# PEER gates inside the activation products: two fp32r products of a split one-hot, two one-hot buffers instead of four

## The chip, the cores and the metric

The kernel runs on one core of one Trainium2 chip. The metric is the device time of one execution in microseconds. The engines are TensorE (PE, with its weight loads as PEld), VectorE (DVE), ScalarE (ACT), GpSimd (POOL) and SyncE (SP), whose queue issues most DMAs.

## What is computed

Two transformer blocks over 256 tokens of width 1024. The change touches the last part alone, the PEER layer of the second block. Cut to that, and written densely as the kernel does it:

```
q  = xn @ w_q                                   # 256 tokens, 8 heads, 2 halves of 128
top 16 of 128 keys per half, top 16 of the 16 x 16 sums per head
idx = i * 128 + j,  gate = softmax(best scores) # 128 experts for each token
act = einsum("cd,ced->ce", xc, u[ic])           # u: 16384 x 1024
hid = gelu(act) * gate
out = einsum("ce,ced->cd", hid, v[ic])          # v: 16384 x 1024
x   = x + out ; rmsnorm(x, norm_f_g)
```

The kernel doesn't gather. It computes `gelu(u @ xn)` for all 16384 experts, keeps it as `A[i, j, token]` (partition i, 128 j, 256 tokens), multiplies it with a dense gate matrix G[i, j, token] that is zero but for the 128 chosen experts, and multiplies the product with all of v. G of one token is a product over the 128 choices k: `sum_k onehot_i[k, i] * gate[k] * onehot_j[k, j]`.

## The kernel before

**Streams.** u and v are each streamed in 64 chunks of 1 MB (`PEER_CHUNKS`, two j of the 128: `CJ = 2`) through three buffers `raw`. The products run in fp32r, so a chunk is split: `lead` is the chunk rounded to fp32r (two buffers), `rest` is what is left (in place, over `raw`). A u chunk takes 48 matmuls of 256 columns on PE: for each of two j, 8 with `nT_hi` and 8 with `nT_lo` on `lead` (L1706), then 8 with `nT_hi` on `rest` (L1710). PE increments `chunk_used` at the chunk's end. ACT turns the bank into gelu values in `A` (L1260, `act_ready`).

**While DVE routes.** DVE does the top-k of the routing during the first `ROUTING = 16` chunks. For these ACT makes `lead` (L1266) and POOL makes `rest` (L974). From chunk 16 on DVE makes both (L2179, L2187). Between chunk 15 and 16 PE waits for DVE's `gates_ready` and turns gates and indices (L1724), which DVE copies into `bestT` and `ijT` (L2190 to L2192, `route_ready`). ACT's exp of the best scores (L1280) stands in ACT's order behind its share of the 16 chunks.

**The gate stage.** It begins when all 64 u chunks are done. The tokens are taken in 64 groups of 4 (`GT`, `GROUPS`), with four buffers `hot` (`HOTS = 4`). For a group, DVE makes the one-hots of j, and in each fourth group those of i too (L2199); ACT makes the other one-hots of i as `relu(1 - (i - iota)^2)` (L1292 four times, L1296). POOL copies four gates (L988) and multiplies the one-hots of j with them (L991). PE does 4 exact fp32 products of 128 columns (L1739; the profile shows 8 records for them), and DVE multiplies the bank into `A` for the group's 4 tokens (L2206, 512 elements a partition).

**The v products** begin when all groups are done (`gated`): 64 chunks, each with 24 matmuls of 512 columns (L1766). DVE makes `lead` and `rest` of v, and `hid_hi` and `hid_lo` of the two columns of `A` (L2230). Then DVE adds the four banks to `h` (L2254), the last norm follows, and the output is stored.

All orders are written out by hand, one in-order queue per engine, held together by semaphores.

Of the kernel before, what the change touches and what calls it, by code (L numbers as in the profile page):

```python
# [27 lines left out]
P = 128  # L28
T = 256
# [65 lines left out]
ROUTING = 16  # L95
# [4 lines left out]
HOTS = 4  # L100
VECTOR_HOTS = 1
SCALAR_HOTS = HOTS - VECTOR_HOTS
# [62 lines left out]
def build(nc, dram, out):  # L165
    with ExitStack() as ctx:
# [21 lines left out]

        h = keep("h", [P, NT, D])
# [180 lines left out]
        bestT = at("bestT", [P, T], WORK + 3072)  # L370
        ijT = at("ijT", [P, 2, T], WORK + 4096)
        hot = [at(f"hot{b}", [P, 2, GT, NKEYS], ARENA + 24576 + 4096 * b) for b in range(HOTS)]
# [7 lines left out]
        cur_g = keep("cur_g", [P, HOTS, GT])  # L380
# [52 lines left out]
        ws_masked = sem("ws_masked")  # L433
# [95 lines left out]
        chunk_used = sem("chunk_used")  # L529
        act_ready = sem("act_ready")  # L530
# [5 lines left out]
        cur_ready = sem("cur_ready")  # L536
# [4 lines left out]
        gain_f_in = sem("gain_f_in")  # L541
# [228 lines left out]
        QUERY_BANK = [4, 5, 6, 7, 0, 1, 2, 3]  # L770
        def fill(i, at_n):

            return 16 * (at_n // RAW_SLOTS + 1) + 16 * (UNROLL // RAW_SLOTS) * i
# [7 lines left out]
        def _(sp):  # L781
# [93 lines left out]
            sp.dma_start(keysT[:, :, :], dram["keysT"].rearrange("c (a n) -> c a n", n=NKEYS)).then_inc(keys_in, 16)  # L875

# [24 lines left out]
            sp.dma_start(gain_f[:, :], dram["norm_f_g"].broadcast_to([P, D])).then_inc(gain_f_in, 16)  # L901
# [7 lines left out]
        def _(pool):  # L909
# [6 lines left out]
            pool.memset(w_sT[CHUNK:P, :, 0:CHUNK], 0.0).then_inc(ws_masked, 1)  # L916

            pool.wait_ge(ws_masked, 1)
# [57 lines left out]

            for n in range(ROUTING % UNROLL):
                pool_rest(n, n)
            with pool.Fori(0, ROUTING // UNROLL) as i:
                for s in range(UNROLL):  # L980
                    at_n = ROUTING % UNROLL + s
                    pool_rest(at_n + UNROLL * i, at_n)

            pool.wait_ge(route_ready, 1)

            def weigh_hot(g, b):
# [7 lines left out]
            with pool.Fori(0, GROUPS // HOTS) as turn:  # L994
                for b in range(HOTS):
                    weigh_hot(HOTS * turn + b, b)
# [3 lines left out]
        def _(act):  # L1000
# [256 lines left out]
            def act_column(n, at_n):  # L1257
                act.wait_ge(chunk_used, n + 1)
                dst = A[:, bass.ds(n * CJ, CJ), :].rearrange("p j t -> p (j t)")
                act.activation(dst, bank[4 + at_n % 2][:, :], ACT.Gelu).then_inc(act_ready, 1)  # L1260
# [6 lines left out]

            head = ROUTING % UNROLL
            for n in range(head):
# [3 lines left out]
            with act.Fori(0, ROUTING // UNROLL) as i:  # L1273
                for s in range(UNROLL):
                    at_n = head + s
# [5 lines left out]
            with act.Fori(ROUTING // 2 - 1, PEER_CHUNKS // 2) as n2:  # L1281
                for b in range(2):
                    act_column(2 * n2 + b, b)

            act.wait_ge(route_ready, 1)

            def scalar_hots(turn, b, peeled):
                k = SCALAR_HOTS * turn + b - VECTOR_HOTS
                if not peeled:
                    act.wait_ge(gates_done, HOTS * (turn - 1) + b + 1)  # L1290
                for t in range(GT):
                    last = act.activation(hot[b][:, 0, t, :], c("iota")[:, 0:NKEYS], ACT.Square,  # L1292
                                          bias=ijT[:, 0, bass.ds((HOTS * turn + b) * GT + t, 1)], scale=-1.0)
                last.then_inc(hot_i_step, 1)
                act.wait_ge(hot_i_step, 2 * k + 1)
                act.activation(hot[b][:, 0, :, :], hot[b][:, 0, :, :], ACT.Relu, bias=1.0,  # L1296
                               scale=-1.0).then_inc(hot_i_step, 1)

            for b in range(VECTOR_HOTS, HOTS):
                scalar_hots(0, b, True)  # L1300
            with act.Fori(1, GROUPS // HOTS) as turn:
                for b in range(VECTOR_HOTS, HOTS):
                    scalar_hots(turn, b, False)
# [4 lines left out]
        def _(pe):  # L1308
# [43 lines left out]
            pe.wait_ge(ws_masked, 1)  # L1352
# [333 lines left out]
            def bank_free(n, peeled):  # L1686
                if not peeled or n >= 2:
                    pe.wait_ge(act_ready, n - 1)

# [5 lines left out]
            def act_split(n, at_n, peeled=False):  # L1695

                slot, b = at_n % RAW_SLOTS, at_n % 2
                bank_free(n, peeled)
                hi = columns_of(lead[b], "u")
                lo = columns_of(rest[slot], "u")  # L1700
                pe.wait_ge(lead_ready, n + 1)
                for j in range(CJ):
                    dst = bank[4 + b][:, j * T:(j + 1) * T]
                    for x in (nT_hi, nT_lo):
                        for k in range(KD):
                            pe.matmul(dst, hi[:, k, j, :], x[:, k, :], start=(x is nT_hi and k == 0), stop=False)  # L1706
                    if j == 0:
                        pe.wait_ge(rest_ready, n + 1)
# [608 lines left out]
```

## Time and profile before

| | |
|---|---|
| median of 3 runs | 1921.12 us (1920.65 to 1923.58) |
| the profiled execution | 1920.95 us, span of the trace 1919.2 us |
| PE busy | 1662.7 us (87%) |
| DVE busy | 1301.7 us (68%) |
| ACT busy | 706.9 us (37%) |
| POOL busy | 451.9 us (24%) |
| the chain that ended last | PE 35%, DVE 7%, issue 3%, POOL 3% |

The time of an execution is the span and about 1.8 us around it. In a timeline row the first number is the start in the span, the second the length, then engine, line, operation, tiles, shapes and count; what stands in brackets is the idle time before it and what ended it. Rows of one engine may overlap by some hundredths to tenths of a microsecond, since an instruction begins before the one ahead has left the pipeline.

### The profile page before, as it was taken

The page shows a single profiled execution, that of the slowest core. Times are in us where ns is not written, and L with a number is a line of the kernel's source. Part 1 is how long each engine was busy: PE and PEld are TensorE (multiplying, and loading weights), DVE is VectorE, ACT ScalarE, POOL GpSimd, SP SyncE. Part 2 cuts the span into 40 slices and gives each one's busy share as a digit, 9 for nine tenths or more (in the row PEclk, how much of TensorE's full clock was granted, in tenths as well). Part 3 has the DMA queues.
Part 4 walks back from the last instruction along what each step waited for, and adds up shares of the span by engine and source line. Part 5 has one row for each costly group of instructions (what it writes and reads, how often), then busy time and mean ns, then how long its engine had stood idle before and what let it go on. Part 6 is the DMA issues. An engine that isn't in the chain of part 4 may idle for free. (4 is left out here: it accounts for less than half of the span.)

```text
span 1919.2 us, 25753 instructions
## 1 busy us (share of the span) xinstructions
PE 1662.7 (87%) x9316; PEld 1331.6 (69%) x9316; DVE 1301.7 (68%) x1434; ACT 706.9 (37%) x929; POOL 451.9 (24%) x257
## 2 busy tenths in 40 slices
PE   6986998788887877788989959999996679999997
PEld 6855555444444536677678959999995568888886
DVE  3345887777777734855216996666659988888887
ACT  4514776666666624243233422222237720000000
POOL 5602111111111105532135840000019930000000
PEclk9996899999999988797999989999999989999999
DMA  8416999999999985421412533555550015555554
GB/s 282 144 50 259 367 397 397 396 396 396 396 396 397 397 324 149 173 89 47 158 37 111 176 131 132 185 187 178 192 176 0 0 66 197 195 188 189 194 196 142
DMA packets 142119, 406.90 MB, mean 212 GB/s; under 512 B 11128, under 2 KB 14328, under 8 KB 125560
## 3 DMA queue, kind: packets, MB, share of 16 engines
q1 hardware_dynamic: 136408, 395.77, 57.3%
q10 hardware_dynamic: 5664, 10.49, 1.5%
q8 instruction: 32, 0.52, 0.1%
q14 instruction: 15, 0.12, 0.0%
HBM read 396.80 MB, written 10.35 MB: 212 GB/s over the span
## 5 line engine op out<-in xcount | busy, mean ns | idle before, releaser
L1983 DVE TENSOR_TENSOR ring_rest<-ring,w_lead 128x2048 fp32r<-128x2048 f32 x128 | 291.7, 2320 | 86.1 <-ACT w_lead L1110 86.0
L1110 ACT ACTIVATE w_lead<-ring 128x2048 fp32r<-128x2048 f32 x128 | 237.8, 1904 | 92.2 <-DMA ring<-in_w_gate 42.9
L2187 DVE TENSOR_TENSOR rest<-raw,lead 128x2048 fp32r<-128x2048 f32 x112 | 256.8, 2293 | 3.9
L2179 DVE CAST lead<-raw 128x2048 fp32r<-128x2048 f32 x112 | 137.4, 1227 | 153.3 <-PE bank L1710 98.9
L711 POOL TENSOR_TENSOR ring_rest<-ring,half_lead 128x2048 fp32r<-128x2048 f32 (+1 forms) x38 | 172.5, 4554 | 233.6 <-ACT half_lead L705 233.5
L1513 PE MATMUL bank<-w_lead,x_two 128*128 128x512 f32 x512 | 154.6, 438 | 56.2 <-ACT w_lead L1110 49.1
L616 ACT ACTIVATE xhat<-h 128x1024 f32<-128x1024 f32 x6 | 6.3, 1056 | 457.0 <-DVE h L2254 360.7
L1513 PE MATMUL bank<-ring_rest,x_two 128*128 128x512 f32 x512 | 149.0, 419 | 29.3 <-DVE ring_rest L1983 29.1
L1513 PEld LDWEIGHTS bank<-w_lead,x_two 128*128 128x128 f32 x512 | 93.7, 200 | 115.8 <-ACT w_lead L1110 87.3
L1766 PE MATMUL bank<-lead,hid_hi 128*128 128x512 f32 x512 | 158.8, 392 | 5.5 <-DVE hid_lo L2230 5.5
L1766 PE MATMUL bank<-rest,hid_hi 128*128 128x512 f32 x512 | 158.6, 391 | 0.0
L1766 PE MATMUL bank<-lead,hid_lo 128*128 128x512 f32 x512 | 158.4, 391 | 0.0
L1706 PE MATMUL bank<-nT_hi,lead 128*128 128x256 f32 x1024 | 145.6, 285 | 4.9 <-ACT lead L1266 2.6
L1513 PEld LDWEIGHTS bank<-ring_rest,x_two 128*128 128x128 f32 x512 | 98.2, 201 | 72.0 <-DVE ring_rest L1983 52.3
L1710 PE MATMUL bank<-nT_hi,rest 128*128 128x256 f32 x1024 | 143.5, 283 | 5.0 <-POOL rest L974 5.0
L1706 PE MATMUL bank<-nT_lo,lead 128*128 128x256 f32 x1024 | 142.4, 281 | 0.0
L954 POOL TENSOR_TENSOR x_two<-x_blk,x_two 128x512 fp32r<-128x512 f32 x32 | 42.4, 1324 | 422.9 <-ACT x_two L1148 422.9
L1706 PEld LDWEIGHTS bank<-nT_hi,lead 128*128 128x128 f32 x1024 | 133.6, 194 | 5.5 <-issue 2.7
L1710 PEld LDWEIGHTS bank<-nT_hi,rest 128*128 128x128 f32 x1024 | 130.6, 189 | 6.0 <-POOL rest L974 6.0
L991 POOL TENSOR_TENSOR hot<-hot,cur_g 128x512 f32<-128x512 f32 x64 | 68.1, 1064 | 282.4 <-DVE hot L2199 277.4
L1706 PEld LDWEIGHTS bank<-nT_lo,lead 128*128 128x128 f32 x1024 | 131.5, 191 | 0.0
L1468 PE MATMUL bank<-ring,hT 128*64 128x512 f32 x512 | 116.9, 598 | 1.4 <-issue 1.4
(317 smaller groups left out, 2710.5 us busy)
## 6 DMA issues: line engine op xcount, KB each, us to landing
ring<-in_w_gate SPq DMA_DIRECT2D x32, 2048.0 KB, 19.7
ring<-in_w_up SPq DMA_DIRECT2D x32, 2048.0 KB, 22.6
ring<-in_w_down SPq DMA_DIRECT2D x32, 2048.0 KB, 20.2
raw<-in_u SPq DMA_DIRECT2D x64, 1024.0 KB, 4.9
raw<-in_v SPq DMA_DIRECT2D x64, 1024.0 KB, 4.9
ring<-in_w_in SPq DMA_DIRECT2D x14, 2048.0 KB, 11.8
ring<-in_w_out SPq DMA_DIRECT2D x4, 2048.0 KB, 7.8
y_sorted<-y_blk ACTq DMA_DIRECT2D x64, 128.0 KB, 5.4
```

The costliest lines, as they stand in the source:

```text
L711: pool.tensor_tensor(half_view(ring_rest[slot], i, half), half_view(ring[slot], i, half), half_lead(i, half).bitcast(F32), ALU.subtract).t ...
L954: pool.tensor_tensor(x_two[j][:, :, BLOCK:], x_blk[j][:, :, :], x_two[j][:, :, 0:BLOCK].bitcast(F32), ALU.subtract).then_inc(x_lo_ready, 1)
L991: pool.tensor_tensor(hot[b][:, 1, :, :], hot[b][:, 1, :, :], spread(cur_g[:, b, :].unsqueeze(2), [P, GT, NKEYS]), ALU.mult).then_inc(hot_j ...
L1110: act.activation(w_lead[half][:, :, :], ring8(slot)[:, 4 * half:4 * half + 4, :], ACT.Copy).then_inc(w_lead_ready, 1)
L1468: last = pe.matmul(dst[half * BLOCK:(half + 1) * BLOCK, :], hidden_t[:, f, :], ring4(w)[:, f, half * 512:(half + 1) * 512], start=(f == 0) ...
L1513: last = pe.matmul(bank[2 * kind + j][:, :], x_two[j][:, 4 * half + k, :], part[:, k, :], start=(ready is w_lead_ready and half == 0 and k ...
L1706: pe.matmul(dst, hi[:, k, j, :], x[:, k, :], start=(x is nT_hi and k == 0), stop=False)
L1710: last = pe.matmul(dst, lo[:, k, j, :], nT_hi[:, k, :], start=False, stop=(k == KD - 1))
L1766: ins = pe.matmul(bank[2 * half + t][:, :], x[b][:, j, tok], v[:, j, half * 512:(half + 1) * 512], start=(first and j == 0 and i == 0), st ...
L1983: dve.tensor_tensor(ring_rest8(slot)[:, part, :], ring8(slot)[:, part, :], w_lead[half][:, :, :].bitcast(F32), ALU.subtract).then_inc(w_re ...
L2179: return dve.tensor_copy(dst, src)
L2187: dve.tensor_tensor(rest[slot][:, :], raw[slot][:, :], lead[b][:, :].bitcast(F32), ALU.subtract).then_inc(rest_ready, 1)
```

## The change

`ROUTING` goes from 16 to 24; POOL makes the rests of 25 chunks (`POOL_RESTS`). ACT makes `lead` for all 64 u chunks, and DVE only `rest` from chunk 25 on. The separate gate stage is gone: chunks 25 to 62 each carry one or two groups (`groups_in`: 12 chunks with one, 26 with two) between their two halves on PE. The one-hots are fp32r, in two buffers. The gates are split too, `best_hi` and `best_lo`; POOL makes two weighted one-hots per group (`hot_hi` and `hot[:, 1]`), and PE does 8 fp32r products of 128 columns where it did 4 fp32 ones. Four banks hold gates, three hold activations.

A column of `A` that isn't computed yet when a group's gates come takes the gates themselves (`tensor_copy`); columns that are there are multiplied. When a later chunk's activations come, ACT writes gelu back into the bank for tokens that already have gates, and DVE multiplies them in (`mix_columns`). The `hot` buffers lie over `h`, so `h` is written to DRAM (`h_kept`, 1 MB) before and read back after the last gates; the load of `gain_f` moves to the end of the u products.

```diff
-ROUTING = 16
+ROUTING = 24
+POOL_RESTS = ROUTING + 1
-HOTS = 4
+HOTS = 2
+GATE_BANKS = 4
+FIRST_MIXED = POOL_RESTS
+LAST_MIXED = PEER_CHUNKS - 2
+def groups_through(n):
+    spans = LAST_MIXED - FIRST_MIXED + 1
+    return min(max(n - FIRST_MIXED + 1, 0), spans) * GROUPS // spans
+def groups_in(n):
+    return range(groups_through(n - 1), groups_through(n))
...
 # sync
+            sp.dma_start(h_kept, h[:, :, :].rearrange("p t d -> p (t d)")).then_inc(h_saved, 16)
...
+            sp.wait_ge(gates_done, GROUPS)
+            sp.wait_ge(h_saved, 16)
+            sp.dma_start(h[:, :, :].rearrange("p t d -> p (t d)"), h_kept).then_inc(final_in, 16)
+            sp.wait_ge(chunk_used, PEER_CHUNKS)
+            sp.dma_start(gain_f[:, :], dram["norm_f_g"].broadcast_to([P, D])).then_inc(final_in, 16)
...
 # gpsimd
-                pool.tensor_copy(cur_g[:, b, :], bestT[:, bass.ds(g * GT, GT)]).then_inc(cur_ready, 1)
-                pool.wait_ge(cur_ready, g + 1)
                 pool.wait_ge(hot_ready, g + 1)
-                pool.tensor_tensor(hot[b][:, 1, :, :], hot[b][:, 1, :, :],
-                                   spread(cur_g[:, b, :].unsqueeze(2), [P, GT, NKEYS]), ALU.mult).then_inc(hot_j_ready, 1)
+                pool.tensor_tensor(hot_hi[b][:, :, :], plain, spread(best_hi[:, tok].bitcast(F32).unsqueeze(2), wide),
+                                   ALU.mult)
+                pool.tensor_tensor(hot[b][:, 1, :, :], plain, spread(best_lo[:, tok].bitcast(F32).unsqueeze(2), wide),
+                                   ALU.mult).then_inc(hot_j_ready, 1)
...
 # scalar
+            for n in range(ROUTING - 1, PEER_CHUNKS):
+                if n + 1 < PEER_CHUNKS:
+                    act.wait_ge(chunk_used, n)
+                    act_lead(n + 1, n + 1, fill(0, n + 1))
+                act_mixed_column(n - 1)
...
+                for g in groups_in(n + 1):
+                    if not vector_makes_both(g):
+                        scalar_hot(g)
...
 # tensor
-                    last = pe.matmul(bank[4 + b][:, t * NKEYS:(t + 1) * NKEYS], hot[b][:, 0, t, :], hot[b][:, 1, t, :],
-                                     start=True, stop=True)
+                    pe.matmul(dst, hot[b][:, 0, t, :], hot_hi[b][:, t, :], start=True, stop=False)
+                    last = pe.matmul(dst, hot[b][:, 0, t, :], hot[b][:, 1, t, :], start=False, stop=True)
                 last.then_inc(gates_done, 1)
...
+            for n in range(ROUTING, PEER_CHUNKS):
...
+                act_half_chunk(n, n, 0)
+                for g in groups_in(n):
+                    gate_products(g)
+                act_half_chunk(n, n, 1).then_inc(chunk_used, 1)
...
 # vector
+            def gate_columns(g, n):
...
+                dve.tensor_copy(A[:, ready:, tok], gates[:, ready:, :])
+                dve.tensor_tensor(A[:, 0:ready, tok], gates[:, 0:ready, :], A[:, 0:ready, tok], ALU.mult).then_inc(gated, 1)
+            def mix_columns(n):
...
+                dve.tensor_tensor(view, pair_of(n)[:, :, 0:done], view, ALU.mult).then_inc(columns_mixed, 1)
...
+            for n in range(FIRST_MIXED, PEER_CHUNKS):
+                if n + 1 < PEER_CHUNKS:
+                    rest_of(n + 1)
+                if n > FIRST_MIXED:
+                    mix_columns(n - 1)
+                else:
+                    dve.wait_ge(act_ready, n)
+                for g in groups_in(n + 1):
+                    one_hots(g)
+                for g in groups_in(n):
+                    gate_columns(g, n)
```

The next two pieces are PE's order where the gates are made. Before, it is the end of the u products: the last half chunk, then the first gate products and the loop over the other groups.

```order
L1706 MATMUL bank<-nT_hi,lead_202 128x256 x8
L1706 MATMUL bank<-nT_lo,lead_202 128x256 x8
L1710 MATMUL bank<-nT_hi,rest_198 128x256 x8
L1726 REGISTER_ALU
L1726 COMPARE_AND_BRANCH
L1739 MATMUL bank<-hot_207 128x128 x4
L1739 MATMUL bank<-hot_208 128x128 x4
L1739 MATMUL bank<-hot_209 128x128 x4
L1739 MATMUL bank<-hot_210 128x128 x4
```

Now, chunk 25, the first with a group (`hot_hi_210` is the upper part of the weighted one-hots, `hot_208` holds the one-hots of i and the lower part):

```order
L1752 MATMUL bank<-nT_hi,rest_199 128x256 x8
L1783 MATMUL bank<-hot_hi_210,hot_208 128x128
L1784 MATMUL bank<-hot_208 128x128
L1783 MATMUL bank<-hot_hi_210,hot_208 128x128
L1784 MATMUL bank<-hot_208 128x128
L1783 MATMUL bank<-hot_hi_210,hot_208 128x128
L1784 MATMUL bank<-hot_208 128x128
L1783 MATMUL bank<-hot_hi_210,hot_208 128x128
L1784 MATMUL bank<-hot_208 128x128
L1748 MATMUL bank<-nT_hi,lead_202 128x256 x8
```

The group's eight products stand between the two halves of the chunk, and the second half can't begin before them.

DVE's order in the u products. Before, for each chunk from 16 on, and in the gate stage for each group:

```order
L2179 CAST lead_202<-raw_195 128x2048
L2187 TENSOR_TENSOR rest_198<-raw_195,lead_202 128x2048
```

```order
L2206 TENSOR_TENSOR A<-bank,A 128x128x4
L2199 ISA
L2199 TENSOR_TENSOR hot_208<-const,ijT 128x512
```

Now one turn in the middle of the u products, with two groups made ready for the next chunk and two gated of the present one:

```order
L2245 TENSOR_TENSOR rest_200<-raw_197,lead_202 128x2048
L2275 TENSOR_TENSOR A<-bank,A 128x2x20
L2254 TENSOR_TENSOR hot_208<-const,ijT 128x512
L2254 TENSOR_TENSOR hot_209<-const,ijT 128x512
L2266 COPY A<-bank 128x72x4
L2267 TENSOR_TENSOR A<-bank,A 128x56x4
```

The rest of the next chunk comes first in each turn, before the one-hots.

## Rows read from the trace of the kernel before

**Rows 1.** Busy time of each engine by stage, the view of windows
```profile
core 0: us, PE busy (x) PEld busy (x) DVE busy (x) ACT busy (x) POOL busy (x), PEclk, DMA share, GB/s
1035.00:1157.10 122.10, 95.71 (x775) 94.13 (x775) 117.81 (x363) 40.71 (x35) 82.10 (x17) 0.91 0.41 138
1157.10:1433.00 275.90, 275.86 (x2304) 275.65 (x2304) 167.63 (x95) 58.95 (x71) 0.00 (x0) 0.99 0.52 179
1433.00:1558.00 125.00, 80.86 (x512) 69.98 (x512) 120.53 (x133) 91.42 (x243) 111.62 (x127) 0.91 0.02 8
1558.00:1909.10 351.10, 351.05 (x1536) 290.12 (x1536) 286.35 (x252) 0.00 (x0) 0.00 (x0) 0.99 0.54 184
```
**Rows 2.** The end of the routing, timeline of DVE and POOL
```profile
1116.77 2.29 DVE L2162 TENSOR_TENSOR match<-const,bdigf 128x2048 f32<-128x2048 f32 x1
1119.10 6.56 DVE L2165 TENSOR_TENSOR match<-match,tif 128x2048 f32<-128x2048 f32 x1
1125.69 2.29 DVE L2166 TENSOR_REDUCE ij<-match 128x128 f32<-128x2048 f32 x1
1128.01 4.27 DVE L2162 TENSOR_TENSOR match<-const,bdigf 128x2048 f32<-128x2048 f32 x1
...
1117.01 13.11 POOL L974 TENSOR_TENSOR rest<-raw,lead 128x2048 fp32r<-128x2048 f32 x2 [1.08 <-ACT lead L1266]
```
**Rows 3.** The same stretch, timeline of PE
```profile
1130.17 1.21 PE L1710 MATMUL bank<-nT_hi,rest 128*128 128x256 f32 x8 [0.65 <-POOL rest L974]
...
1153.24 0.69 PE L1724 MATMUL bank<-const,best 128*128 128x128 f32 x2 [19.00 <-DVE best L2175]
...
1157.10 2.08 PE L1706 MATMUL bank<-nT_hi,lead 128*128 128x256 f32 x8 [2.31 <-DVE lead L2179]
...
1161.73 1.12 PE L1706 MATMUL bank<-nT_hi,lead 128*128 128x256 f32 x8
...
1164.59 1.12 PE L1706 MATMUL bank<-nT_hi,lead 128*128 128x256 f32 x8
```
**Rows 4.** One turn of the gate stage, timeline of all engines
```profile
1500.63 1.13 PE L1739 MATMUL bank<-hot 128*128 128x128 f32 x8 [0.91 <-POOL hot L991]
1500.73 1.26 ACT L1292 ACTIVATE hot<-const,ijT 128x128 f32<-128x128 f32 x4
1500.86 0.68 DVE L2206 TENSOR_TENSOR A<-bank,A 128x512 f32 x1
1501.06 1.04 POOL L991 TENSOR_TENSOR hot<-hot,cur_g 128x512 f32<-128x512 f32 x1
1501.45 1.19 DVE L2199 TENSOR_TENSOR hot<-const,ijT 128x512 f32<-128x512 f32 x1
1502.03 0.63 ACT L1296 ACTIVATE hot<-hot 128x512 f32<-128x512 f32 x1
```
**Rows 5.** Instructions by tile, ns min/median/max: the tile hot
```profile
L2199 DVE TENSOR_TENSOR hot<-const,ijT x64: 677/1192/1726, 1433.1 to 1547.5; 128x512 f32<-128x512 f32 x48, 128x1024 f32<-128x1024 f32 x16
```
**Rows 6.** Groups by line and shape, busy us and mean ns
```profile
L2187 DVE TENSOR_TENSOR rest<-raw,lead 128x2048 fp32r<-128x2048 f32 x112 | 256.8, 2293 | 3.9
L954 POOL TENSOR_TENSOR x_two<-x_blk,x_two 128x512 fp32r<-128x512 f32 x32 | 42.4, 1324 | 422.9 <-ACT x_two L1148 422.9
L1266 ACT ACTIVATE lead<-raw 128x2048 fp32r<-128x2048 f32 x16 | 30.4, 1908 | 0.0
```
**Rows 7.** Narrow matmuls of the MoE part, timeline of PE
```profile
400.61 1.10 PE L1454 MATMUL bank<-const,hid 64*128 64x64 f32 x8
```
**Rows 8.** End of the u products, timeline of all engines
```profile
1431.85 1.11 PE L1710 MATMUL bank<-nT_hi,rest 128*128 128x256 f32 x8
1433.06 3.87 DVE L2199 TENSOR_TENSOR hot<-const,ijT 128x1024 f32<-128x1024 f32 x4 [7.86 <-PE bank L1710]
```
**Rows 9.** Begin and end of the v products, timeline of all engines
```profile
1558.04 1.19 PE L1766 MATMUL bank<-lead,hid_hi 128*128 128x512 f32 x2 [5.52 <-DVE hid_lo L2230]
...
1909.13 2.48 DVE L2254 TENSOR_TENSOR h<-bank,h 128x512 f32<-128x512 f32 x4 [6.01 <-PE bank L1766]
```

More of the change, by code:

```diff
@@ L99, with vector_makes_both @@
 GROUPS = T // GT
-HOTS = 4
-VECTOR_HOTS = 1
-SCALAR_HOTS = HOTS - VECTOR_HOTS
+HOTS = 2
[7 more added lines that the diff above has]
+    return range(groups_through(n - 1), groups_through(n))
+def vector_makes_both(g):
+    return g % 4 == 0
+SCALAR_TURN = {g: k for k, g in enumerate(g for g in range(GROUPS) if not vector_makes_both(g))}
 PAIR = [(0, 0), (0, 1), (0, 2), (1, 0), (1, 1), (1, 2)]
@@ L1280, in _, with act_mixed_column @@
             act.activation(best[:, :, :], best[:, :, :], ACT.Exp).then_inc(best_exp, 1)
[L1281 to L1290, printed above, removed]
+            def act_mixed_column(n):
+                done = GT * groups_through(n)
+                act.wait_ge(chunk_used, n + 1)
+                pair = pair_of(n)
+                if done < T:
+                    last = act.activation(A[:, n * CJ:(n + 1) * CJ, done:], pair[:, :, done:], ACT.Gelu)
+                if done:
+                    last = act.activation(pair[:, :, 0:done], pair[:, :, 0:done], ACT.Gelu)
+                last.then_inc(act_ready, 1)
@@ L1294, in scalar_hots @@
                 last.then_inc(hot_i_step, 1)
                 act.wait_ge(hot_i_step, 2 * k + 1)
-                act.activation(hot[b][:, 0, :, :], hot[b][:, 0, :, :], ACT.Relu, bias=1.0,
+                act.activation(hot[b][:, 0, :, :], hot[b][:, 0, :, :].bitcast(F32), ACT.Relu, bias=1.0,
                                scale=-1.0).then_inc(hot_i_step, 1)
[L1299 to L1303, printed above, removed]
+            for n in range(ROUTING - 1, PEER_CHUNKS):
[3 more added lines that the diff above has]
+                act_mixed_column(n - 1)
+                if n + 1 == FIRST_MIXED:
+                    act.wait_ge(h_saved, 16)
+                    act.wait_ge(route_ready, 1)
+                for g in groups_in(n + 1):
+                    if not vector_makes_both(g):
+                        scalar_hot(g)
@@ L1713, in _, with act_chunk @@
+            def act_chunk(n, at_n, peeled=False):
+                if not peeled or n >= 3:
+                    pe.wait_ge(act_ready, n - 2)
+                act_half_chunk(n, at_n, 0)
+                act_half_chunk(n, at_n, 1).then_inc(chunk_used, 1)
             pe.wait_ge(score_ready, 8)
-            for n in range(ROUTING % UNROLL):
-                act_split(n, n, True)
-            with pe.Fori(0, ROUTING // UNROLL) as i:
+            for n in range(UNROLL):
+                act_chunk(n, n, True)
@@ new lines, in _, with rest_of, one_hots @@
+            dve.tensor_copy(ijT[:, 0, :], bank[ROUTE_BANK[0]][:, T:])
+            dve.tensor_copy(ijT[:, 1, :], bank[ROUTE_BANK[1]][:, 0:T]).then_inc(route_ready, 1)
+            def rest_of(n):
+                slot, b = n % RAW_SLOTS, n % 2
+                dve.wait_ge(lead_ready, n + 1)
+                dve.tensor_tensor(rest[slot][:, :], raw[slot][:, :], lead[b][:, :].bitcast(F32), ALU.subtract).then_inc(rest_ready, 1)
+            def one_hots(g):
+                b = g % HOTS
+                first = 0 if vector_makes_both(g) else 1
@@ L2213, in _ @@
[L2213 to L2223 removed]
+                if n > FIRST_MIXED:
+                    dve.wait_ge(columns_mixed, n - FIRST_MIXED)
```

172 lines of the change are left out of this document (84 added, 88 removed).

## The prediction

> **What bounds the kernel now.** I read the chain that ended last first, and then cut the PEER part into its stages with the view of windows [rows 1]. In the u products from chunk 16 on and in the v products PE is busy for all of the stretch, at full clock: these two stages are PE's own time. The two others are not. In the gate stage (1433 to 1558) PE is busy for 81 of 125 us, while DVE has 120.5 and POOL 111.6: DVE and POOL set it, some 1.9 us for each of 64 groups. In the routing stage PE has 95.7 of 122.1 us: the timeline of PE shows that it finished its 16 chunks at about 1134 (1130.17 and 32 matmuls) and sat for 19 us until DVE's routing was through [rows 3]. So there are two things to win, the idle part of the routing and the gate stage, and the change goes for both.
>
> Two prices of PE come from here. The half chunks begin 2.86 us apart (1161.73, 1164.59) [rows 3]: 24 matmuls of 256 columns at 0.119 us, 5.71 us a chunk. The v products take 351.1 us for 64 chunks, and 10.1 us follow them [rows 9].
>
> **A lock between DVE and POOL.** In the timelines DVE's operations with two operands in SBUF and POOL's don't overlap in substance. L2165 alone is a 2.3 us operation like L2162; it took 6.56 us when POOL had just begun a rest, and POOL's two rests took 13.1 us between them [rows 2]. In the gate stage a one-hot of DVE took 1.19 us beside POOL's multiply, and the same takes 0.68 where POOL is idle [rows 4, 5]. L2206, which reads PSUM and one SBUF operand, keeps its 0.68 us beside POOL, and L2166, with one operand, its 2.29 [rows 2, 4]. So each waits for the whole instruction of the other. The Trainium skill says so too (SBUF: State Buffer, Who interferes with whom: an exclusive lock, the second one blocks fully, and a VectorE instruction with at most one SBUF input doesn't contend); the trace agrees, and as a rule it speaks against this change, which puts DVE's rests and POOL's multiplies into the same stretch.
>
> **Routing, 24 chunks.** Before, chunk 16 starts at 1157.1 [rows 3]. Now PE goes on to chunk 23 before the turn. But POOL's rests go on too, beside DVE's last 2-input operations. At 1132.3 (1128.01 and 4.27) five of these are left, three L2165 and two L2162; the reduction L2166 runs under a rest. One rest and one such operation take 6.6 us together (from the end of L2165 at 1125.7 to 1132.3, or 13.1 over two), so some 4.5 for the rest. Five turns bring DVE to 1165.5, the last L2166 to 1167.8, and the small subtraction waits for the next rest until 1170.0. PE in this time gets a rest each 6.6 us in place of 5.7: those of chunks 16 to 21 end at 1136.8 to 1170.0. 22 follows at 1174.9 and 23 at 1180.9 (its lead waits for chunk 21, at 1173.8, and takes 0.5 for the gelu before it and 1.9 us [rows 6]). A chunk ends 3.8 us or more after its rest came, chunk 22 at 1179.5 and chunk 23 at 1185.2. ACT's exp now stands behind the lead of chunk 23, near 1177, and DVE's gates are ready at about 1182, hidden behind chunk 23. With 1.6 us for the turn chunk 24 starts at 1186.8. Eight chunks more have then cost 29.7 us in place of 45.7: 16 us won. Without any waits for POOL it would be 1181.
>
> **The gates on PE.** What a fp32r product of 128 columns costs no row shows. From below: the slope between 256 columns (0.119) and 512 (351.1 / 1536 = 0.229) leaves 0.064. But the 64-column matmuls of the MoE part, with a full 128-column weight load for each, start (1.10 - 0.27) / 7 = 0.118 us apart, where 0.27 is one of them to its end [rows 7]: a floor by the weight load. From above: eight records of L1739 take 1.13 us in a row [rows 4], 0.12 apart, and these are exact products in two records each; if a narrow fp32r product cost as much as an exact one, a group would be 1.9 to 2.3 us. I take the floor, 8 x 0.119 = 0.95 us, since L1454 is the same limit with still fewer columns. The Trainium skill would have less (TensorE: Matmul & The Clock Gate, Back-to-back issue gap: about 81 ns for a pair of load and matmul with 128 columns); by it 64 groups would be 41 us and not 61, and the whole up to 19 us shorter, less what then waits for POOL. No run here shows it. PE's own sum: 40 chunks x 5.71 = 228.2, and 64 x 0.95 = 60.9: 289.1 us.
>
> **Do the others keep up?** A chunk has 6.66 us with one group and 7.61 with two. ACT: lead 1.9, gelu 0.8, two times 1.26 and 0.63 [rows 4, 6]: 6.5 us, enough. DVE: rest 2.2, one-hots 0.6 each, gates 0.7 per group in two instructions (533 ns of elements, as L2206), columns 0.2 to 0.6: some 5.4. POOL: four multiplies. The nearest row is L991 with 1.04 us, the same multiply with the same broadcast operand and a plain f32 result [rows 4]; L954, a subtraction of whole tiles into fp32r, has 1.27 at best and 1.32 in the mean [rows 6]. Those are the two bounds; I take 1.04, 0.98 in a row.
>
> The sums fit, but the order doesn't quite. Take a chunk n with one group, its start as zero, followed by one with two. ACT starts the lead a little after (DVE and ACT begin 0.1 us after the last matmul's end [rows 8]) and ends at 2.0. DVE's rest runs to 4.3, columns to 4.7, two one-hots to 5.9. POOL's four multiplies would end at 6.9, 7.9, 8.8 and 9.8. Chunk n+1 starts at 6.66, its turn of DVE asks for the next rest at 8.75, gets the port after the third multiply and holds it to 11.0; the fourth ends at 12.0. PE wants it after half a chunk and one group, at 6.66 + 2.85 + 0.95 = 10.5. It waits 1.6 us, and behind it stands the second half of the chunk. With 1.27 us a multiply the third ends at 9.5, the rest at 11.7, the fourth at 12.9: 2.5 us. After a chunk with two groups DVE asks a microsecond later, the fourth multiply is already on, and nothing waits. There are 12 chunks with one group, so 12 stalls: 19 to 30 us. Lateness goes on in part to the next one-hots, as there are two buffers only; I take 24.
>
> **Start of v.** Before, PE sat 5.5 us after the last group and the v products began at 1558.0 [rows 9]. Now chunk 63 has no gates, and lead, rest and hidden of v chunk 0 are made under it. For v chunk 1 DVE must first mix columns 63: 0.2 + 0.8 (gelu) + 0.6, then lead 1.2, rest 2.2 and hidden 1.1, 6.3 us after the end of u, against 5.5 of the first v chunk: 0.9 us. The load of `h` runs under chunk 63 and `gain_f` beside v chunk 2, hidden unless that load comes over 2 us late.
>
> **The sum**, against the profiled execution: 1186.8 + 289.1 + 24 + 0.9 = 1500.8 where it was 1558.0; then 351.1 + 10.1: a span of 1862.0. It had 1919.2 of 1920.95 us, so 1863.8 us; the profiled execution lies 0.2 us from the median, so the prediction is 1864, 57 us less.
>
> **Rivals.**
> - PE alone sets the stage: the multiplies slip in between and no stall is left. For it: the sums of all engines fit. Against it: the lock, and a deadline missed by 1.6 us. 24 us less and up to 4 in the routing: 1836 to 1840.
> - The serial loop is worse than I drew it: a multiply costs 1.3 us, or each of the 26 chunks with two groups waits 2 us. ACT's hidden waits and POOL's own issue time speak for it, the slack after chunks with two groups against it. 40 to 60 us of stalls: 1880 to 1900.
> - A narrow fp32r product costs as an exact fp32 one. For it: no fp32r row has under 256 columns. Against it: nothing in the trace asks for it. At 1.9 us a group the stage is 228.2 + 121.6 and 1901 comes out; at 2.3 us it is 375 and 1926, slower than before. It decides from 2.2 us a group on (1921.1 - 1.75 - 361.2 - 0.9 - 1186.8 - 228.2 = 142.3, over 64), 0.278 us a product.
> - The change does what it says but the routing gives nothing, DVE being held longer by the lock: chunk 24 at 1200, 1877. In the range.
>
> **Chances.** Forecast, 1850 to 1882, 0.60. PE alone, and all under 1850, 0.15. Worse loop 0.15. Costly narrow products 0.10, of which half slower than before. The range from 1842 to 1898 leaves some 2 in 10 out. Anything within 0.2% (3.8 us, what can be told from no change here) of before has 0.02; faster 0.93, slower 0.05.
>
> **What would show it.** PE's records of L1783 and L1784: 0.119 us apart, or not. The gate stage gone, and PE busy for some 290 of 315 us between its turn (near 1185) and the first v product (near 1501). Waits of PE for POOL's second multiply, about 12 of some 2 us, in chunks that follow one with one group. The three last multiplies of match on DVE at 6.6 us each with their wait. PE's turn without a wait before it. The prediction is wrong if a multiply takes much over 1.3 us, if PE waits for ACT or for the gate banks, or if the products are not at the weight load's floor.

## The result and the profile after

| | before | after |
|---|---|---|
| median | 1920.88 us (4 runs, 1917.83 to 1923.58) | 1868.01 us (4 runs, 1866.38 to 1870.25) |
| ratio to before, 95% interval | | 0.9726 (0.9707 to 0.9745) |
| the profiled execution | 1920.95 us | 1870.25 us, span of the trace 1868.5 us |

The change makes the kernel 52.9 us faster; 1864 us had been predicted. First the page of the kernel after: busy time of each engine, the granted clock in 40 slices, and the chain that ended last.

```profile
PE 1650.7 (88%) x9316; PEld 1328.3 (71%) x9316; DVE 1249.8 (67%) x1481; ACT 765.7 (41%) x990; POOL 560.9 (30%) x266
...
PEclk9997999999999998978989999999998999999999
...
PE 30%; POOL 10%; issue 5%; ACT 1%; DVE 1%; DMA 1%; DVEq 0%; POOLq 0%; SPq 0%; ACTq 0%
```

POOL, with 3% of the chain before, now has 10%, and POOL's rests and its two multiplies are what stands behind it. Four windows of the kernel after: chunks 0 to 23, chunk 24 to the end of u, the v products, and ten microseconds out of the second one. They answer to [rows 1]; the columns are the same.

```profile
1029.62:1180.42 150.80, 141.98 (x1158) 139.70 (x1159) 136.42 (x358) 61.64 (x52) 133.66 (x25) 0.99 0.45 161
1180.42:1508.94 328.52, 305.84 (x2435) 303.99 (x2434) 216.51 (x277) 185.98 (x357) 168.94 (x129) 0.94 0.38 131
1508.94:1858.41 349.47, 348.94 (x1536) 288.03 (x1536) 287.14 (x254) 1.80 (x3) 0.00 (x0) 1.00 0.54 188
1270.00:1280.00 10.00, 8.08 (x44) 7.94 (x43) 5.25 (x8) 4.52 (x11) 6.29 (x5) 0.66 0.09 37
```

The gate stage is gone. The second window ought to be PE's own, but PE is busy for 305.8 of 328.5 us at a mean clock of 0.94: something makes PE wait, and something slows it while it works. The last window, with a clock of 0.66, is one of the places where both happen.

**The routing** [rows 2, 3]. Timeline of DVE, ACT and PE of the kernel after, from the last large operations to chunk 24.

```profile
1113.70 6.56 DVE L2211 TENSOR_TENSOR match<-match,tif 128x2048 f32<-128x2048 f32 x1
...
1126.92 6.58 DVE L2211 TENSOR_TENSOR match<-match,tif 128x2048 f32<-128x2048 f32 x1
...
1164.54 0.42 DVE L2217 TENSOR_TENSOR best<-best,best_sum 128x256 f32<-128x256 f32 x1
...
1172.45 0.42 ACT L1313 ACTIVATE best<-best 128x256 f32<-128x256 f32 x1
...
1179.85 0.38 PE L1771 MATMUL bank<-const,best 128*128 128x128 f32 x2
...
1180.42 1.20 PE L1748 MATMUL bank<-nT_hi,lead 128*128 128x256 f32 x8
```

DVE's multiplication of `match` (L2211, before L2165) takes 6.6 us at 1113.7, 1126.9, 1140.2 and 1153.4, each time behind a rest of POOL. The small subtraction (L2217) is done at 1165.0, ACT's exp at 1172.9, and the turn (L1771) has no bracket: PE doesn't wait for the routing at all, where it waited 19.00 us before.

**The gates.** Instructions of the kernel after by the tile `hot`, then its waits from 1180 to 1510 (us in total, times, longest).

```profile
L1783 PE MATMUL bank<-hot_hi,hot x256: 222/277/473, 1189.1 to 1499.6; 128*128 128x128 f32 x128
...
L2254 DVE TENSOR_TENSOR hot<-const,ijT x64: 675/852/1778, 1182.4 to 1493.3; 128x512 fp32r<-128x512 f32 x48, 128x1024 fp32r<-128x1024 f32 x16
L1027 POOL TENSOR_TENSOR hot_hi<-hot,best_hi x64: 1032/1040/2957, 1183.7 to 1495.9; 128x512 fp32r<-128x512 f32 x64
L1029 POOL TENSOR_TENSOR hot<-hot,best_lo x64: 1032/1039/3147, 1186.6 to 1496.9; 128x512 fp32r<-128x512 f32 x64
```
```profile
POOL hot_hi L1027 <- DVE hot L2254: 148.6, 41, 9.6
DVE rest L2245 <- ACT lead L1300: 101.6, 38, 6.2
...
PE bank L1783 <- POOL hot L1029: 22.4, 12, 2.3
```

The fp32r multiply costs POOL 1.04 us, as the f32 one did [rows 4]. PE waits twelve times for the lower part of a weighted one-hot, 22.4 us in all. Timeline of one such wait:

```profile
1352.41 1.04 POOL L1029 TENSOR_TENSOR hot<-hot,best_lo 128x512 fp32r<-128x512 f32 x1
...
1353.40 1.03 POOL L1027 TENSOR_TENSOR hot_hi<-hot,best_hi 128x512 fp32r<-128x512 f32 x1
...
1354.30 2.29 DVE L2245 TENSOR_TENSOR rest<-raw,lead 128x2048 fp32r<-128x2048 f32 x1 [2.10 <-ACT lead L1300]
1354.40 3.09 POOL L1029 TENSOR_TENSOR hot<-hot,best_lo 128x512 fp32r<-128x512 f32 x1
...
1357.55 0.33 PE L1783 MATMUL bank<-hot_hi,hot 128*128 128x128 f32 x1 [1.54 <-POOL hot L1029]
```

POOL is at the end of the third of a chunk's four multiplies when DVE's next rest begins at 1354.30. The fourth takes 3.09 us in place of 1.04: it stands behind the rest. PE wants its result at 1355.84 and gets it at 1357.55.

This is chunk 45, a two-group chunk behind a one-group chunk. In chunk 26, which is of the same kind, the order came out the other way. Timeline of POOL and DVE:

```profile
1194.86 1.04 POOL L1029 TENSOR_TENSOR hot<-hot,best_lo 128x512 fp32r<-128x512 f32 x1
1194.94 3.10 DVE L2245 TENSOR_TENSOR rest<-raw,lead 128x2048 fp32r<-128x2048 f32 x1 [2.28 <-ACT lead L1300]
```

Here the fourth multiply begins 0.08 us ahead of the rest, it is the rest that stands behind, and PE doesn't wait. The wait comes one chunk later, in chunk 27, where a rest (1202.42) gets ahead of the fourth multiply (1202.71, again 3.09 us). Counted through from chunk 25, eight of the twelve waits lie in the first two-group chunk behind a one-group chunk (32, 35, 41, 45, 51, 54, 57, 60) and four in the one after it (27, 30, 39, 49). In those four the fourth multiply had begun 0.01 to 0.40 us ahead of the rest in the chunk before.

**What comes after a wait.** The next timeline is PE's, from another of the twelve.

```profile
1270.08 0.27 PE L1784 MATMUL bank<-hot 128*128 128x128 f32 x1
1272.28 0.47 PE L1783 MATMUL bank<-hot_hi,hot 128*128 128x128 f32 x1 [1.92 <-POOL hot L1029]
1272.55 0.41 PE L1784 MATMUL bank<-hot 128*128 128x128 f32 x1
...
1274.04 2.02 PE L1748 MATMUL bank<-nT_hi,lead 128*128 128x256 f32 x8
1275.85 1.91 PE L1748 MATMUL bank<-nT_lo,lead 128*128 128x256 f32 x8
1277.56 1.71 PE L1752 MATMUL bank<-nT_hi,rest 128*128 128x256 f32 x8
1279.10 1.12 PE L1748 MATMUL bank<-nT_hi,lead 128*128 128x256 f32 x8
```

After this wait the products start 0.21 us apart and not 0.11, and eight matmuls of 256 columns take 2.02 us and not 1.12. The granted clock has gone from 2.4 to 1.2 GHz, for most of the second half of the chunk. From the wait's end to the next chunk PE needs 3.77 us at full clock (0.89 for a group, 2.88 for 24 matmuls and the changes between). Worked out from PE's timeline for all twelve:

| wait ends at | wait, us | to the next chunk, us | over 3.77 |
|---|---|---|---|
| 1205.85 | 1.73 | 5.36 | 1.6 |
| 1230.85 | 1.73 | 5.41 | 1.6 |
| 1248.59 | 1.88 | 3.84 | 0.1 |
| 1272.28 | 1.92 | 6.82 | 3.1 |
| 1306.47 | 1.98 | 6.80 | 3.0 |
| 1325.25 | 1.54 | 5.36 | 1.6 |
| 1357.55 | 1.54 | 3.84 | 0.1 |
| 1389.04 | 2.26 | 3.85 | 0.1 |
| 1405.49 | 2.16 | 6.78 | 3.0 |
| 1432.37 | 2.19 | 6.92 | 3.2 |
| 1458.92 | 1.70 | 5.37 | 1.6 |
| 1483.96 | 1.75 | 3.85 | 0.1 |

Eight of twelve waits are followed by the lower clock, and it costs about 1.5 or 3.0 us over the 0.08 of the others, 18.0 us together. The length of the wait doesn't sort them: the longest (2.26) has no slow stretch, one of the shortest (1.54) has one. Restarting PE is a third part: from product to product a wait adds 0.16 us more than its own length, and 0.08 come behind it, 2.9 us over twelve. With PE's own time at full clock (40 chunks, 228.2, and 512 products at 0.111, 56.8, together 285.0) the stage comes to 285.0 + 22.4 + 2.9 + 18.0 = 328.3 us, and it has 328.5.

**Start and end of v** [rows 9], timeline of the kernel after.

```profile
1508.94 0.70 PE L1812 MATMUL bank<-lead,hid_hi 128*128 128x512 f32 x2 [0.31 <-DVE hid_lo L2300]
...
1858.41 2.48 DVE L2325 TENSOR_TENSOR h<-bank,h 128x512 f32<-128x512 f32 x4 [6.20 <-PE bank L1812]
```

### The profile page after: what moved, and what is told of

Read it like the earlier page. It is cut to its first block and busy times, and to the rows that moved or that the text cites. A ratio compares the mean times of both kernels' runs of the same rounds, so it can differ in the third digit from the quotient of the medians.

```text
span 1868.5 us, 24876 instructions
## 1 busy us (share of the span) xinstructions
PE 1650.7 (88%) x9316; PEld 1328.3 (71%) x9316; DVE 1249.8 (67%) x1481; ACT 765.7 (41%) x990; POOL 560.9 (30%) x266
## 5 line engine op out<-in xcount | busy, mean ns | idle before, releaser
L2245 DVE TENSOR_TENSOR rest<-raw,lead 128x2048 fp32r<-128x2048 f32 x39 | 96.6, 2477 | 101.6 <-ACT lead L1300 101.6
L1300 ACT ACTIVATE lead<-raw 128x2048 fp32r<-128x2048 f32 x64 | 122.4, 1913 | 90.6 <-PE bank L1752 89.6
L1748 PE MATMUL bank<-nT_hi,lead 128*128 128x256 f32 x1024 | 152.3, 293 | 2.6 <-ACT lead L1300 2.6
L2233 DVE TENSOR_TENSOR rest<-raw,lead 128x2048 fp32r<-128x2048 f32 x64 | 146.8, 2294 | 2.2
L1748 PE MATMUL bank<-nT_lo,lead 128*128 128x256 f32 x1024 | 147.6, 288 | 0.0
L1011 POOL TENSOR_TENSOR rest<-raw,lead 128x2048 fp32r<-128x2048 f32 x25 | 134.2, 5375 | 34.5 <-ACT lead L1300 33.6
L1748 PEld LDWEIGHTS bank<-nT_hi,lead 128*128 128x128 f32 x1024 | 137.8, 200 | 2.7 <-issue 2.7
L1748 PEld LDWEIGHTS bank<-nT_lo,lead 128*128 128x128 f32 x1024 | 136.7, 198 | 0.0
## 6 DMA issues: line engine op xcount, KB each, us to landing
ring<-in_w_gate SPq DMA_DIRECT2D x32, 2048.0 KB, 19.7
```

What stands on the lines that cost most here:

```text
L1011: pool.tensor_tensor(rest[slot][:, :], raw[slot][:, :], lead[b][:, :].bitcast(F32), ALU.subtract).then_inc(rest_ready, 1)
L1300: act.activation(lead[b][:, :], raw[slot][:, :], ACT.Copy).then_inc(lead_ready, 1)
L2233: dve.tensor_tensor(rest[slot][:, :], raw[slot][:, :], lead[b][:, :].bitcast(F32), ALU.subtract).then_inc(rest_ready, 1)
L2245: dve.tensor_tensor(rest[slot][:, :], raw[slot][:, :], lead[b][:, :].bitcast(F32), ALU.subtract).then_inc(rest_ready, 1)
```

## The experiments

After the result my theory was this. PE waits for the fourth multiply of a two-group chunk, because a whole rest of DVE is held in front of it (I took it to be the first such chunk behind each one-group chunk); and the wait costs twice, once itself and once by the clock behind it. The main rival was that the low clock comes and goes by itself, or with the new mix of matmuls, and that the waits are only the 22 us that I see. Others: that the fp32r split is what costs (its products, or its extra work), and that the gain lies in the routing alone.

**Exact products.** The split is taken out: one-hots in f32, POOL multiplies once, PE does four exact fp32 products a group (eight records of 128 columns).

```diff
-                pool.tensor_tensor(hot_hi[b][:, :, :], plain, spread(best_hi[:, tok].bitcast(F32).unsqueeze(2), wide),
-                                   ALU.mult)
-                pool.tensor_tensor(hot[b][:, 1, :, :], plain, spread(best_lo[:, tok].bitcast(F32).unsqueeze(2), wide),
+                pool.tensor_tensor(hot[b][:, 1, :, :], plain, spread(best_hi[:, tok].unsqueeze(2), wide),
...
-                    pe.matmul(dst, hot[b][:, 0, t, :], hot_hi[b][:, t, :], start=True, stop=False)
-                    last = pe.matmul(dst, hot[b][:, 0, t, :], hot[b][:, 1, t, :], start=False, stop=True)
+                    last = pe.matmul(dst, hot[b][:, 0, t, :], hot[b][:, 1, t, :], start=True, stop=True)
```

> The changed kernel with the interleaving and the rest kept, but the gates as one exact fp32 product (4 a group) of one weighted one-hot, so POOL has one multiply a group and not two. My theory: the 12 waits of PE for POOL's last multiply (22 us) go, and with them the stretches at the lower clock behind them (some 20 us); the products cost 0.119 us a record where the fp32r ones cost 0.111 (+4 us): about 1830. Rival, the lower clock comes from the narrow matmuls themselves and not from the waits: about 1850. Rival, the split into fp32r products is what makes the gates cheap on PE: over 1868, as an exact group would be near 1.9 us (+60, less the waits).

Measured: 1831.20 us (1828.24 to 1832.01), ratio 0.9537 (0.9522 to 0.9553). The window of its mixed stage, chunk 24 to the first v product, and PE's timeline at one two-group chunk:

```profile
1183.52:1469.25 285.73, 285.42 (x2435) 285.24 (x2434) 197.43 (x276) 185.36 (x357) 81.11 (x65) 1.00 0.43 151
```
```profile
1306.58 1.95 PE L1779 MATMUL bank<-hot 128*128 128x128 f32 x16
1308.28 1.20 PE L1744 MATMUL bank<-nT_hi,lead 128*128 128x256 f32 x8
```

PE is busy for 285.4 of 285.7 us at full clock, with no wait for POOL. The stage is 42.8 us shorter than that of the kernel after, which is its waits, restarts and low clock together (43.3). Two things follow. Some 43 us of the stage are no work of PE's. And the exact product is as cheap as the two fp32r ones: sixteen records lie within 1.70 us, 0.106 each. The split brings nothing here, and it costs POOL the second multiply.

**Second group later.** PE does the second group of a chunk 16 matmuls (1.9 us) later, between the products of `lead` and those of `rest` in the second half. Work and multiplies stay the same.

```diff
-                for g in groups_in(n):
+                groups = list(groups_in(n))
+                for g in groups[:1]:
                     gate_products(g)
-                act_half_chunk(n, n, 1).then_inc(chunk_used, 1)
+                act_half_chunk(n, n, 1, groups[1:]).then_inc(chunk_used, 1)
```

> The changed kernel, but PE does the second group of a chunk 16 matmuls (1.9 us) later, inside the chunk's second half. My theory: the deadline of POOL's last multiply moves 1.9 us and nearly all of the 12 waits go, with the lower clock behind them: about 1828. Rival, the clock isn't tied to the waits: about 1847. Rival, the wait is moved on, since the next one-hots of ACT and DVE wait for these products too: 1860 or more.

Measured: 1833.73 us (1830.35 to 1836.39), ratio 0.9555 (0.9538 to 0.9572). Its mixed stage and the one kind of wait that is left for the gates:

```profile
1183.86:1471.62 287.76, 286.81 (x2436) 285.46 (x2433) 221.47 (x277) 185.31 (x357) 172.54 (x129) 1.00 0.42 150
```
```profile
PE bank L1785 <- POOL hot L1029: 0.5, 2, 0.3
```

POOL still has both multiplies (172.5 us busy), but its result is only wanted later. 22 us of waits go, and the stage gets 40.8 us shorter: the clock came back with them. The total lies 6 us over what I expected: chunk 24 starts 3.4 us later than in the kernel after, and the stage has 2.8 us more than PE's own time.

**Useless work in place of the wait.** In the twelve two-group chunks behind a one-group chunk PE does 12 matmuls of 256 columns into an unused bank before the second group. This adds work and leaves nothing out. The edit takes these for the twelve chunks in which PE waited. Eight of them are; in the other four (26, 29, 38, 48) the filling stands one chunk ahead of the wait.

```diff
+                    if i and len(groups_in(n - 1)) == 1:
+                        for _ in range(FILL):
+                            pe.matmul(bank[3][:, 0:T], columns_of(lead[n % 2], "u")[:, 0, 1, :], nT_hi[:, 0, :],
+                                      start=True, stop=True)
                     gate_products(g)
```

> The changed kernel with 12 useless matmuls of 256 columns (1.4 us, into a free bank) ahead of the second group in each of the 12 chunks in which PE waits. They do work that nobody needs in a time in which PE sat idle. My theory, that an idle PE of some 1.9 us is followed by a stretch at the lower clock, which costs some 20 us in all: the waits shrink to 0.5 us, the end of each stays where it was, the clock stays up: about 1848. Rival, the clock is lowered by something else: 1868, no change.

Measured: 1854.79 us (1853.90 to 1857.51), ratio 0.9663 (0.9646 to 0.9679). The timeline shows what one filling costs, the window the stage, the waits what is left:

```profile
1203.29 1.64 PE L1797 MATMUL bank<-nT_hi,lead 128*128 128x256 f32 x12
1204.77 0.22 PE L1784 MATMUL bank<-hot_hi,hot 128*128 128x128 f32 x1
```
```profile
1187.23:1495.22 307.99, 304.74 (x2580) 302.74 (x2578) 213.72 (x277) 186.12 (x357) 164.29 (x129) 1.00 0.39 139
```
```profile
PE bank L1784 <- POOL hot L1030: 2.7, 6, 0.7
```

This tells the two readings of the clock apart. The waits in chunks 27, 30, 39 and 49 are gone too, and the six that are left are 0.7 us or less. The filling costs 12 x 1.48 = 17.8 us of PE and takes 19.7 us of waits away, and 1.4 us with the six restarts that went; if the low clock had nothing to do with the waits, the stage would be 2 to 3 us shorter. It is 20.5 us shorter (308.0 for 328.5), and the stage's clock is at 1.00. The difference, 17 to 19 us, is what the table above gives for the low clock (18.0). The stage's clock is at 1.00 too in every other run whose waits are gone or no longer than 1.2 us, with as many records of 128 columns in each. So the waits bring the clock down, and a kernel that does useless work in them is 9 to 13 us faster than one that waits (against the two medians of the kernel after, 1863.7 and 1868.0). The span gained 7.7 us less than the stage: chunk 0 started at 1034.6 and not 1029.6, which is 5.0 of them, the 24 chunks took 1.8 us more and what follows the stage 0.9.

**Only the routing.** The kernel before, with 22 chunks under the routing in place of 16 (the change has 24).

```diff
-ROUTING = 16
+ROUTING = 22
```

> The kernel before with ROUTING 22 in place of 16, nothing else: the routing part of the change alone (22, since 24 doesn't fit its loops). My theory: six more chunks are done while DVE routes, at 6.6 us each by the lock with POOL's rests and with DVE's routing later by it; chunk 22 starts near 1176 where it was 1191: 14 us less, about 1906. Rival, the lock gives it all back: 1919 or more.

Measured: 1902.04 us (1900.50 to 1904.11), ratio 0.9908 (0.9891 to 0.9924), 16.9 us less than before. PE's timeline:

```profile
1128.17 1.21 PE L1710 MATMUL bank<-nT_hi,rest 128*128 128x256 f32 x8 [0.65 <-POOL rest L974]
...
1134.78 1.21 PE L1710 MATMUL bank<-nT_hi,rest 128*128 128x256 f32 x8 [0.65 <-POOL rest L974]
...
1171.78 0.38 PE L1724 MATMUL bank<-const,best 128*128 128x128 f32 x2
...
1174.91 1.28 PE L1706 MATMUL bank<-nT_hi,lead 128*128 128x256 f32 x8 [2.31 <-DVE lead L2179]
```

One chunk in 6.6 us while DVE's large operations last, no wait at the turn, and 2.31 us for DVE's first `lead`. Chunk 22 starts at 1174.9, where six more chunks behind [rows 3] would have put it at 1157.1 + 34.3 = 1191.4. So 16.5 us were won, 2.1 of them because chunk 0 started earlier in this execution. Of the change's 52.9 us, between a quarter and a third is the routing (14.4 to 16.9 us).

**The kernel after again**, unchanged, beside the next two on the same chip.

> The changed kernel once more, with nothing altered, as a measure beside the next two on the same chip and to see whether the 12 waits and the stretches at the lower clock come back: 12 waits of 1.5 to 2.3 us for POOL's last multiply, between 5 and 12 of them followed by a slow stretch; 1866 to 1870. If the slow stretches are an accident of one execution, there are none or few and it's near 1850.

Measured: 1863.72 us (1859.95 to 1867.46), ratio 0.9702 (0.9678 to 0.9725). Its mixed stage and its waits:

```profile
1183.55:1504.14 320.59, 298.57 (x2436) 296.73 (x2433) 214.16 (x277) 186.04 (x357) 169.46 (x129) 0.96 0.38 134
```
```profile
PE bank L1783 <- POOL hot L1029: 21.7, 12, 2.2
```

Twelve waits again, eleven of them at the same places in the order and with the same lengths to 0.02 us. The one of 2.26 us in chunk 49 is now one of 1.58 us in chunk 48: there the fourth multiply had begun ahead of the rest, and this time the rest was ahead by 0.14 us. Only five have a slow stretch behind them (those that end at 1209.0, 1250.2, 1322.5, 1356.3 and 1476.1, by 1.6, 1.6, 3.2, 1.6 and 3.1 us). Their 10.8 us (over the same 0.08) with 285.0, 21.7 and 2.9 make 320.4, and the stage has 320.6. So the waits are in the main the program's, and the number of slow stretches is the execution's: 7.2 of the 7.9 us between these two stages, and the shorter waits the other 0.7.

**The rest in two halves.** DVE subtracts 1024 elements twice, so that POOL's multiply can come between them.

```diff
-                dve.tensor_tensor(rest[slot][:, :], raw[slot][:, :], lead[b][:, :].bitcast(F32), ALU.subtract).then_inc(rest_ready, 1)
+                for part in (slice(0, 1024), slice(1024, 2048)):
+                    last = dve.tensor_tensor(rest[slot][:, part], raw[slot][:, part], lead[b][:, part].bitcast(F32),
+                                             ALU.subtract)
+                last.then_inc(rest_ready, 1)
```

> The changed kernel with DVE's rest in the mixed chunks in two instructions of 1024 elements instead of one of 2048. DVE's work is the same, 0.07 us more for the second instruction. My theory, a lock held for one whole instruction: POOL's last multiply gets in between the halves, comes 1.1 us earlier, the 12 waits shrink from 1.9 to 0.8 us, and the lower clock comes seldom or never: 1835 to 1842. Rival, DVE and POOL share a port by its bandwidth: how the work is cut doesn't matter, 1866 to 1870.

Measured: 1845.99 us (1843.46 to 1848.98), ratio 0.9616 (0.9597 to 0.9635). One of its waits in the timeline, then the waits and the stage:

```profile
1205.63 3.53 DVE L2246 TENSOR_TENSOR rest<-raw,lead 128x1024 fp32r<-128x1024 f32 x2 [1.10 <-ACT lead L1300]
1206.06 2.02 POOL L1029 TENSOR_TENSOR hot<-hot,best_lo 128x512 fp32r<-128x512 f32 x1
1208.13 0.19 PEld L1783 LDWEIGHTS bank<-hot_hi,hot 128*128 128x128 f32 x1 [0.94 <-POOL hot L1029]
1208.13 0.33 PE L1783 MATMUL bank<-hot_hi,hot 128*128 128x128 f32 x1 [0.80 <-POOL hot L1029]
```
```profile
PE bank L1783 <- POOL hot L1029: 10.8, 15, 1.2
```
```profile
1183.64:1483.26 299.62, 288.47 (x2436) 286.21 (x2434) 224.51 (x316) 186.07 (x357) 159.84 (x129) 1.00 0.41 144
```

The multiply gets in after the first half and takes 2.0 and not 3.1 us, while DVE's two halves take 3.53 and not 2.3. The port is therefore held for one instruction and passed on between two. I had expected 1835 to 1842: the waits got shorter, but there are fifteen, since three more chunks now have one, and chunk 24 starts 3.2 us later than in the kernel after. All are 1.2 us or less, and none has a slow stretch behind it: all 15 need 3.84 to 3.86 us to the next chunk.

**DVE makes the upper part.** The split stays; of the two multiplies, DVE takes `hot_hi`, right behind its one-hots, and POOL keeps the other.

```diff
-                pool.wait_ge(hot_ready, g + 1)
-                pool.tensor_tensor(hot_hi[b][:, :, :], plain, spread(best_hi[:, tok].bitcast(F32).unsqueeze(2), wide),
-                                   ALU.mult)
+                pool.wait_ge(hot_ready, 2 * g + 2)
...
+                dve.wait_ge(hot_ready, 2 * g + 1)
+                dve.tensor_tensor(hot_hi[b][:, :, :], hot[b][:, 1, :, :].bitcast(F32),
+                                  spread(best_hi[:, g * GT:(g + 1) * GT].bitcast(F32).unsqueeze(2), [P, GT, NKEYS]),
+                                  ALU.mult).then_inc(hot_ready, 1)
```

> The changed kernel with both fp32r products kept, but DVE makes the upper weighted one-hot (0.6 us) where POOL did (1.04), so POOL has one multiply a group. My theory: POOL's work for a chunk with two groups ends before DVE asks for the port again, no wait is left, and DVE has some 6.3 us of 7.5 to do: 1827 to 1832, as with the exact product. Rival, DVE becomes the bound: its turns come too late for POOL and PE, 1850 or more.

Measured: 1832.53 us (1828.35 to 1833.36), ratio 0.9537 (0.9519 to 0.9556). The multiply on DVE, by tile, and the stage:

```profile
L2256 DVE TENSOR_TENSOR hot_hi<-hot,best_hi x64: 691/693/1416, 1188.7 to 1457.9; 128x512 fp32r<-128x512 f32 x64
```
```profile
1185.46:1470.94 285.48, 285.17 (x2436) 285.00 (x2434) 262.97 (x341) 185.68 (x357) 82.26 (x65) 1.00 0.43 151
```

The same 512 elements take DVE 0.69 us and POOL 1.04. With DVE at 263 of 285 us PE waits for no multiply any more, and the stage is the same as with exact products. So it wasn't the split. Nor was it the amount of work on the port, which the run with the second group later left as it was. It was the fourth multiply of POOL, which missed its deadline by 1.5 to 2.3 us because a rest of 2.3 us stood ahead of it.

## Why the prediction was right, and what it missed

1864 us were predicted and 1868.0 measured, in the likeliest of the cases, with its mechanism. But 4 us (6.5 in the profiled execution) are closer than the working deserves, and that is luck: one term of 18.0 us is missing altogether, and six others that came out smaller made up for most of it. What waiting cost in all, 43.3 us, is the size of the "worse loop", though not by its mechanism.

- **Routing: right.** 24 chunks took 150.8 us (1029.62 to 1180.42), predicted were 151.7 (1035.1 to 1186.8). The cadence of 6.6 us and the turn without a wait came as drawn. The exp was done at 1172.9 and not near 1177, mostly because the whole part began 5.4 us earlier. The 0.9 us less are in the turn, which took 0.57 us for the 1.6 predicted.
- **Products: right, a little too dear.** 0.111 us apart and not 0.119, 4.1 us over 512. I had assumed a floor by the weight load. The spacing fits it, being about that of the 64-column matmuls in [rows 7], but no run changed the load alone, so the floor isn't shown. The rule that spoke for less, about 81 ns for a pair (the Trainium skill, TensorE: Matmul & The Clock Gate, Back-to-back issue gap), doesn't hold for these products. The Trainium skill, the same page under LDWEIGHTS, gives the time of a load as its columns over 1.2, in ns; for 128 columns that is an estimate of 107 ns. The trace is near it, with 0.106 to 0.111 us between products.
- **Waits: right in number, size and cause, wrong in part in their place.** There are twelve of 22.4 us together; I took 24, and the order of events (third multiply, rest, fourth multiply, PE) is that of the timeline. But four of them lie in a two-group chunk behind a two-group chunk, where I had said that nothing waits. My drawing had DVE ask 0.05 us before the third multiply ended; in chunks 26, 29, 38 and 48 the fourth multiply got in first, and the wait moved on by a chunk. That the count is still twelve wasn't foreseen. Restarting PE after the waits costs another 2.9 us that I had not counted.
- **The missing term: the clock behind the waits**, 18.0 us in the profiled execution. I had said that PE would be busy "for some 290 of 315 us" and took full clock for it. In [rows 1] the routing and the gate stage, where PE waits, stand at 0.91, and in [rows 3] the first eight matmuls after the turn took 2.08 us, for 1.12 at full clock. I read these as costs of single long waits and put no price on twelve short ones. The Trainium skill (the same page, HAM oscillation) describes a kernel whose PE waits in each step and begins every next one cold. Its waits are longer than these, and the table above agrees only in part: the clock was low behind 8 waits of 12 and, in the second execution, behind 5.
- **Start of v.** 0.3 us of waiting before the first product and 0.4 before the third chunk, for the 0.9 predicted before the second (its steps add up to 6.1 us and not 6.3, so to 0.6 or 0.7). The v products took 349.5 and not 351.1 us, as PE no longer sat 5.5 us before them and did not begin at the low clock (the first two matmuls take 0.70 us for 1.19). This is another piece of the clock that I had carried over unseen.
- **Ahead of the change.** Chunk 0 began at 1029.6 us and in before's trace at 1035.1, though nothing was changed there. In the other runs it lies between 1031.0 and 1034.7, whatever the kernel. A sum that begins at chunk 0 of one trace is uncertain by these 5 us.

The sum, span against span: -5.4 (start of chunk 0), -0.9 (24 chunks), +14.5 for the mixed stage (products -4.1, waits -1.6, restarts +2.9, start of v -0.6, clock +18.0, which is 14.6), -1.6 (v). That is 6.6 us over the 1862.0 predicted, by rounded terms, and the trace has 1868.5. The terms that I had not counted are 20.9 us, and those that I had too dear, with the earlier start, 14.2.

Of the rivals, "PE alone" lost here, but the experiments reach it: without the waits the kernel takes 1831 to 1834 us. That is under the 1836 to 1840 that I gave it, since that sum had the dearer products, the cold start of v and chunk 24 at 1186.8, where these runs have 1183.5 to 1185.5. The "worse loop" did not come: a multiply into fp32r takes 1.04 us, and of the chunks with two groups twelve had a wait and not all 26. The narrow product isn't dear: it and the exact one start at the same pace, 0.106 to 0.111 us a record. What stays open is why one wait is followed by the lower clock and the next one isn't; no run here tells.

## What to carry to other kernels

Price a wait of PE by what follows it as well: waits of 1.5 to 2.3 us cost here 1.6 to 1.9 times what the profile shows as waiting (43.3 for 22.4 us with restart and clock in one execution, 35.4 for 21.7 in another), and in a tight loop it can pay to move the work that is waited for two microseconds later, or even to fill the gap with useless matmuls.

Where DVE and POOL both use two operands in SBUF, look at the order of their instructions and not at their sums: an instruction of 1 us that is wanted soon must not stand behind one of 2.3. Where the two ask within some tenths of a microsecond, either order can come out, and a wait can move from one turn of the loop to the next.

Before splitting a small product into two fp32r ones, look whether the exact one isn't already as cheap.

## What the runs showed of the hardware

- The granted clock falls from 2.4 to 1.2 GHz behind some waits of PE as short as 1.54 us (8 of 12 waits, and 5 of 12 in a second execution, all of 1.54 to 2.26 us), and stays there so long that about 1.5 or 3.0 us are lost. Behind fifteen waits of 1.20 us or less in one execution, and six of 0.71 or less in another, it never fell.
- Products of 128 columns, each with its own weight load, start 0.111 us apart in fp32r at full clock and 0.21 at the lower one; an exact fp32 product of the same size costs two such records, 0.106 each.
- A subtraction of 2048 elements on DVE with two operands in SBUF (2.29 us) holds up POOL's multiply behind it, which then takes 3.09 us and not 1.04. Cut into two of 1024, it lets the multiply in between: 2.02 us for the multiply, 3.53 for the two halves.
- POOL's multiply of 512 elements with a broadcast operand takes 1.04 us, whether it writes f32 or fp32r; DVE's takes 0.69 us.
